# Two-block transformer on one core: the second block's norms, output projections and routing rearranged

## What is computed

```python
h = concat(meta, x)                                  # (272, 1024)
for i in range(2):
    if i == 0:                                       # short convolution
        b, c, u = split(rmsnorm(h, g_mix[0]) @ w_in, 3)
        h = h + (b * conv3(c * u)) @ w_out
    else:                                            # latent attention, 8 heads
        a = rmsnorm(h, g_kv) @ w_dkv                 # keys and values
        cq = rmsnorm(rmsnorm(h, g_mix[1]) @ w_dq, g_cq)
        h = h + attention(cq @ w_uq, a, w_ukv) @ w_o
    h = h + hier_moe(rmsnorm(h, g_ffn[i]))           # 64 experts in 8 groups
return rmsnorm(h, g_final)[:, 16:]

def hier_moe(x):       # x (272, 1024)
    # logits = x @ [w_grp, w_exp] (72 columns): the best group of 8, in it the best 2 experts
    # each expert: (silu(x @ w_gate) * (x @ w_up)) @ w_down, hidden width 256, 3 MB of weights
```

## Time and profile before

| | us |
|---|---|
| median of 3 runs | 2895.99 (2892.11 to 2897.56) |
| the profiled execution | 2896.46 |
| its span | 2894.7 |
| TensorE busy in the span | 2553.1 (88%) |
| VectorE busy | 701.9 (24%) |
| ScalarE busy | 346.7 (12%) |

### The profile page before, as it was taken

One profiled execution on the slowest core, in us unless ns is written; L12 is line 12 of the kernel. 1 busy time (PEld: TensorE's weight loads), 2 busy tenths in 40 slices (PEclk: granted clock), 3 DMA queues, 4 the chain that ended last, 5 costly groups with the idle time before them and its releaser, 6 DMA issues.

```text
span 2894.7 us, 30016 instructions
## 1 busy us (share of the span) xinstructions
PE 2553.1 (88%) x11566; PEld 1550.9 (54%) x11566; DVE 701.9 (24%) x1516; ACT 346.7 (12%) x770; POOL 35.7 (1%) x57
## 2 busy tenths in 40 slices
PE   7999779998999968999897888889869869888887
PEld 5776447774777545777573433434335534443433
DVE  1111521112111352111222323232221133223232
ACT  2001211002000222000200011111102100111011
POOL 0000000000000000000000000000000000000000
PEclk9999879999999968999998799999977678999999
DMA  8432405434552322342514499999740046999995
GB/s 283 160 131 102 146 0 175 149 116 150 177 174 102 133 85 88 131 165 102 168 59 174 198 422 422 422 421 422 312 154 1 1 181 289 422 422 422 422 422 224
DMA packets 206424, 618.45 MB, mean 214 GB/s; under 512 B 14941, under 2 KB 122150, under 8 KB 156950
## 3 DMA queue, kind: packets, MB, share of 16 engines
q1 hardware_dynamic: 200022, 610.89, 54.5%
q0 software_dynamic: 1600, 5.06, 0.5%
q10 hardware_dynamic: 4736, 1.58, 0.2%
HBM read 616.44 MB, written 1.05 MB: 213 GB/s over the span
## 4 chain that ended last, share of the span: by engine, by line
issue 68%; PE 14%; DMA 11%; DVE 2%; PEld 1%; POOL 1%; SPq 1%; ACT 1%; DVEq 0%; ACTq 0%; POOLq 0%; PEldq 0%
DMA ring<-expert_parts 11%; PE PS L1051 3%; PE PS L1127 3%; PE PS L1071 1%; PE PS L1100 1%; PE PS L596 1%; PEld PS L1071 1%; SPq L761 1%; PE PS L543 1%; POOL small L1243 1%; PE PS L578 1%; PE PS L1116 1%; PE PS L579 1%; PE PS L1823 1%; ACT xn L1286 0%
## 5 line engine op out<-in xcount | busy, mean ns | idle before, releaser
L1862 PE MATMUL PS<-xT,ring 128*128 128x256 f32 x2816 | 628.8, 382 | 11.7 <-DVE xT L1526 9.8
L1862 PEld LDWEIGHTS PS<-xT,ring 128*128 128x128 f32 x2816 | 538.8, 192 | 121.2 <-issue 49.1
L1127 PE MATMUL PS<-ring,arena 128*32 128x512 f32 x2048 | 269.7, 676 | 82.2 <-DMA ring<-expert_parts 79.4
L1872 PE MATMUL PS<-ring,arena 128*128 128x512 f32 x704 | 316.1, 592 | 0.0
L1100 PE MATMUL PS<-arena,xn 128*128 128x128 f32 (+1 forms) x1632 | 298.0, 313 | 6.8 <-DVE arena L993 6.8
L1100 PEld LDWEIGHTS PS<-arena,xn 128*128 128x128 f32 (+1 forms) x1632 | 236.3, 195 | 98.4 <-issue 37.3
L1127 PEld LDWEIGHTS PS<-ring,arena 128*32 128x32 f32 x2048 | 70.0, 122 | 273.1 <-issue 168.3
L1547 DVE TENSOR_TENSOR arena<-PS,rb 128x256 f32<-128x256 f32 x88 | 37.4, 425 | 726.3 <-PE PS L1862 725.6
L1116 PE MATMUL PS<-arena 128*128 128x512 f32 (+1 forms) x408 | 199.1, 610 | 7.8 <-DVE h L1009 5.2
L1872 PEld LDWEIGHTS PS<-ring,arena 128*128 128x128 f32 x704 | 133.4, 190 | 132.9 <-issue 126.7
L1009 DVE TENSOR_TENSOR h<-h,PS 128x1024 f32<-128x1024 f32 (+1 forms) x102 | 123.9, 1215 | 309.5 <-PE PS L1116 309.5
(11 more groups left out here) (310 smaller groups left out, 1722.2 us busy)
## 6 DMA issues: line engine op xcount, KB each, us to landing
ring<-expert_parts SPq DMA_DIRECT2D x384, 1024.0 KB, 15.5
ring<-ffn_gate_up SPq DMA_DIRECT2D x88, 1024.0 KB, 7.6
ring<-ffn_down SPq DMA_DIRECT2D x44, 1024.0 KB, 9.8
ring<-w_in SPq DMA_DIRECT2D x16, 768.0 KB, 5.3
ring<-conv_w_in SPq DMA_DIRECT2D x12, 1024.0 KB, 11.7
ring<-w_out SPq DMA_DIRECT2D x8, 768.0 KB, 5.8
ring<-ple_gate SPq DMA_DIRECT2D x8, 768.0 KB, 5.6
rows<-norm_gains POOLq DMA_DIRECT2D x8, 512.0 KB, 8.6
```

The costliest lines, as they stand in the source:

```text
L1127: last = mm(PS[BLK * j:BLK * (j + 1), 2, :], lhsT=xgT[:, k, j * BLK:(j + 1) * BLK], rhs=gu[j][:, k, :], start=k == 0, stop=k == KD - 1)
L1862: last = mm(PS[:, 4 + local % 4, s * 256:(s + 1) * 256], lhsT=w[:, s, k, j * P:(j + 1) * P], rhs=xT[:, k, META:T2], start=k == 0, stop=k = ...
L1872: return mm(PS[:, 2 * t + n, :], lhsT=hid[:, j, t * P:(t + 1) * P], rhs=w[:, j, n * 512:(n + 1) * 512], start=first, stop=final, skip_grou ...
```

## The change

1. Transposes take raw rows of `h` in halves (`h2_turn`), as the halves are updated; ScalarE and VectorE copy them with the gain (`h2_copied`, `meta_copied`, `last_quarter`). 1/rms (`h2_rstd`) is applied to the products: the convolution's by a spread row vector `rb3` and its square `rb3sq`, the latents and the logits by a scalar per row.
2. The output projections (`out_projection`, `out_act`, `out_vec`) work tile by tile. The meta rows' 16 products are made on four column strips of 32 and folded by two products with a constant. The logits are made inside, between the transposes.
3. The scaled rows for the selection are written by ScalarE after the logits' inputs are made; features are in plain order for the logits.
4. Counts take four wider products in place of nine, with two sums by VectorE. The copy of gathered rows is in halves.
5. After each expert loop the combines use banks of their own; in the last layer the meta tile is left out, and squares, 1/rms, scaling and store go tile by tile.

```diff
+        def h2_copied(b, turned_at, t, n, bank, gain):
+            act = nc.scalar
+            act.wait_ge(S.h2_turned, H2_TURNED[b] + turned_at)
+            for k in range(4):
+                last = act.activation(xT[:, 4 * n + k, xcol(t)], PS[:, bank, k * P:(k + 1) * P], ACT.Copy,
+                                      scale=gain[:, 4 * n + k:4 * n + k + 1])
+            last.then_inc(S.h2T_act, 1)
+        def h2_square(b, half_at, t, n):
+            act = nc.scalar
+            if half_at is not None:
+                act.wait_ge(S.h2_half, H2_HALF[b] + half_at)
+            pr, c = (META, slice(0, D)) if t == 2 else (P, slice(512 * n, 512 * n + 512))
+            return act.activation(xn[0:pr, t, c], h[0:pr, t, c], ACT.Square, scale=1.0 / 32, accum_out=ssq[0:pr, n, t:t + 1])
+        def meta_copied(dve, b, turned_at, bank, outs):
+            dve.wait_ge(S.h2_turned, H2_TURNED[b] + turned_at)
+            for dst, gain in outs:
+                last = nc.vector.tensor_tensor(dst[:, :, 0:META], PS[:, bank, 0:KD * META].rearrange("p (k w) -> p k w", w=META),
+                                               gain.unsqueeze(2).to_broadcast([P, KD, META]), ALU.mult)
+            last.then_inc(S.h2T_vec, 1)
+        def last_quarter(dve, b, turned_at, gain):
+            dve.wait_ge(S.h2_turned, H2_TURNED[b] + turned_at)
+            nc.vector.tensor_tensor(xT[:, 4:8, xcol(1)], PS[:, 3, :].rearrange("p (k w) -> p k w", w=P),
+                                    gain[:, 4:8].unsqueeze(2).to_broadcast([P, 4, P]), ALU.mult).then_inc(S.h2T_vec, 1)
+        def h2_rstd(dve, b, r):
+            dve.wait_ge(S.h2_sq, b + 1)
+            nc.vector.scalar_tensor_tensor(ms[:, 0:3], ssq[:, 0, :], EPS, ssq[:, 1, :], ALU.add, ALU.add).then_inc(S.ms_ready, 1)
+            dve.wait_ge(S.rstd_ready, r + 1)
+        def h2_turn(b, t, n, bank, half_at):
+            pe = nc.tensor
+            if b:
+                pe.wait_ge(S.h2_half, H2_HALF[b] + half_at)
...
+                for k in range(4):
+                    last = pe.transpose(PS[:, bank, k * P:(k + 1) * P], h[:, t, (4 * n + k) * P:(4 * n + k + 1) * P], ident)
+            last.then_inc(S.h2_turned, 1)
+        def out_projection(pe, i, src, slots):
...
+            for n in range(2):
+                products(0, n, range(KD - 1))
+            if i == 0:
+                pe.wait_ge(S.conv_ready, KD)
+            for n in range(2):
+                products(0, n, [KD - 1]).then_inc(S.out_done, 1)
+            for n in range(2):
+                for c in range(2):
+                    for j in range(4):
+                        last = mm(PS[32 * j:32 * j + 32, 4 + n, :], lhsT=src[:, 2 * j + c, 0:32], rhs=w[n][:, 2 * j + c, :],
+                                  start=c == 0, stop=c == 1)
+                        if n == c == 1:
+                            last.then_inc(S.strips_done, 1)
+            products(1, 0, range(KD)).then_inc(S.out_done, 1)
+            pe.drain().then_inc(slot_free[i][slots[0]], 1)
+            pe.wait_ge(S.const2_loaded, 16)
+            pe.wait_ge(S.strips_copied, i + 1)
+            for n in range(2):
+                last = mm(PS[0:META, 6 + n, :], lhsT=cst("fold"), rhs=strips[:, n, :], start=True, stop=True)
+            last.then_inc(S.out_done, 1)
+            for n in range(2):
+                h2_turn(b, 0, n, n, n + 1)
+            products(1, 1, range(4))
+            h2_turn(b, 2, 0, 6, 4)
+            h2_turn(b, 1, 0, 2, 3)
+            products(1, 1, range(4, KD)).then_inc(S.out_done, 1)
+            pe.drain().then_inc(slot_free[i][slots[1]], 1)
+            pe.wait_ge(M[i].router_loaded, 48)
+            pe.wait_ge(S.h2T_act, H2T_ACT[b] + 2)
+            logits(0)
+            pe.wait_ge(S.h2T_vec, H2T_VEC[b] + 1)
+            logits(2)
+            pe.wait_ge(S.h2T_act, H2T_ACT[b] + 3)
+            h2_turn(b, 1, 1, 3, 5)
+            logits(1, range(4))
+            pe.wait_ge(S.h2T_vec, H2T_VEC[b] + 2)
+            logits(1, range(4, KD)).then_inc(M[i].pe_step, 1)
...
         def second_act(act, norm):
             act.wait_ge(S.h_upd, 9)
             act.dma_start(const2, A["const_table2"]).then_inc(S.const2_loaded, 16)
             router_loads(act, 0)
-            norm(8, 3)
+            gain = cols("norm_mix_g_2", 8)
+            for u, (t, n) in ((1, (0, 0)), (2, (0, 1)), (4, (1, 0))):
+                h2_copied(0, u, t, n, 2 * t + n, gain)
+            for t in range(2):
+                act.wait_ge(S.h_half, 16 * DEPTH + 2 * t + 2)
+                for n in range(2):
+                    h2_square(0, None, t, n)
+            h2_square(0, None, 2, 0).then_inc(S.h2_sq, 1)
...
             def gathered(n):
-                dve.wait_ge(M[i].selected, n + 1)
-                v_.tensor_tensor(xgT, PS[:, 0:2, :].rearrange("p a (k w) -> p (a k) w", w=P),
-                                 gk.unsqueeze(2).to_broadcast([P, KD, P]), ALU.mult).then_inc(M[i].xgT_ready, 1)
+                for half in range(2):
+                    ks = slice(HALF * half, HALF * half + HALF)
+                    dve.wait_ge(M[i].selected, 2 * n + half + 1)
+                    v_.tensor_tensor(xgT[:, ks], PS[:, half, :].rearrange("p (k w) -> p k w", w=P),
+                                     gk[:, ks].unsqueeze(2).to_broadcast([P, HALF, P]), ALU.mult).then_inc(M[i].xgT_ready, 1)
...
-            for t in range(3):
-                combine(groups, t)
+            pe.wait_ge(M[i].xgT_ready, 2 * groups + 2)
+            for t, bank in ((0, 6), (1, 0), (2, 2))[0:3 - i]:
+                combine(groups, t, bank)
```

More of the change, by code:

```diff
@@ L425, in build @@
         convT = take(2180, [KD, T2])
+        rb3, rb3sq = arena[:, 4400:4400 + T2], arena[:, 4672:4672 + T2]
+        diag3 = take(4944, [3, P])
+        strips = take(5400, [2, 512])
         wr = take(11400, [KD, NG + NE])
@@ L432, in build @@
         e1, e2, msel, rsel, ta, tb = [take(1100 + 192 * i, [3, NE]) for i in range(6)]
+        sums = take(1100 + 192 * 2, [5, NE])
         thr = take(2252, [NE, 8])
@@ L787, in experts, with second_pool @@
             return groups
[L789 to L798 removed]
+        def second_pool(pool, rstd, power):
+            for r in range(28, 34):
+                rstd(r, 3)
+            for t in range(2):
+                power(34 + t, rs[:, t:t + 1], ms[:, t:t + 1], 1)
+        H2_HALF = {1: 0, 2: 5, 3: 10, 4: 15}
@@ new lines, in out_projection, with products, logits @@
+        def out_projection(pe, i, src, slots):
+            mm = nc.tensor.matmul
+            b = 2 * i + 1
+            w = [slot_w(j, KD, 512) for j in slots]
+            def products(t, n, ks):
+                for k in ks:
+                    last = mm(PS[:, 2 * t + n, :], lhsT=src[:, k, xcol(t)], rhs=w[n][:, k, :], start=k == 0, stop=k == KD - 1)
+                return last
+            def logits(t, ks=range(KD)):
+                r = META if t == 2 else P
+                for k in ks:
+                    last = mm(PS[0:r, 4, t * (NG + NE):(t + 1) * (NG + NE)], lhsT=xT[:, k, xcol(t)], rhs=wr[:, k, :],
+                              start=k == 0, stop=k == KD - 1)
+                return last
+            for n in range(2):
[35 more added lines that the diff above has]
+            logits(1, range(4, KD)).then_inc(M[i].pe_step, 1)
@@ new lines, in out_act @@
+        def out_act(act, i, gain):
+            b = 2 * i + 1
+            act.wait_ge(S.strips_done, 4 * i + 4)
+            nc.scalar.activation(strips, PS[:, 4:6, :], ACT.Copy).then_inc(S.strips_copied, 1)
+            for n in range(2):
+                h2_square(b, n + 1, 0, n)
+            for n in range(2):
+                h2_copied(b, n + 1, 0, n, n, gain)
+            h2_square(b, 3, 1, 0)
+            h2_square(b, 4, 2, 0)
+            h2_copied(b, 4, 1, 0, 2, gain)
+            h2_square(b, 5, 1, 1).then_inc(S.h2_sq, 1)
@@ L1052, in second_pe @@
                                   start=k == 0, stop=k == KD - 1)
+                    if x == 0 and s == 1:
+                        pe.wait_ge(S.diag_ready, 3 * DEPTH + 1)
+                        for t in range(3):
+                            r = META if t == 2 else P
+                            spread_ = mm(PS[:, 7, xcol(t)], lhsT=cst("ones")[0:r, :], rhs=diag3[0:r, t, 0:r], start=True, stop=True)
+                        spread_.then_inc(S.r_done, 1)
                 last.then_inc(S.conv_products, 1)
@@ L1435, in _ @@
                 ple(l)
-            second_act(act, norm, squares)
+            second_act(act, norm)
         @block.vector
```

296 lines of the change are left out of this document (173 added, 123 removed).

## The result

The changed kernel takes 2811.24 us (median of 4 runs, 2807.77 to 2813.31), the kernel before 2894.05 us in the same comparison: ratio 0.9715, 95% interval 0.9695 to 0.9734. The forecast was 2818 in 2800 to 2838, and faster. The profiled execution took 2813.31 us with a span of 2811.6, against 2896.46 and 2894.7: 83.1 us of span to explain, and I forecast 78.

What follows compares the result with a forecast made beforehand. Expert-weight DMA was taken to bound the loops, so only the serial stretches around them gain. Terms summed to 80.2 us, less 2 for hops gives 78; from the median 2895.99 that forecasts 2818 us, range 2800 to 2838.

Steps and rivals of the forecast that it cites:

- The frame: Loops and first block: DMA sets the loops' length, they stay unchanged, and time saved before or between them counts in full.
- A: Entry of the second block: products start 7.0 us earlier, less 1.0 for the spread and 3 for clock; gain 3 us.
- B: First output projection, last convolution product to last logit: 70.8 us become 43, a gain of 27.8 us (21 to 29).
- D: Second output projection up to the last logit: 66.1 us become 43, a gain of 23.1 us (16 to 24).
- C: Routing in both layers: fewer count instructions and a shorter wait before the expert products, a gain of 3.4 us.
- E: Attention's entry: products start 13.6 us earlier and first ones run 2.3 faster at 2.4 GHz; gain 15.9 us (11 to 16).
- F: Tail: no meta tile, norm and store tile by tile, half the bytes in the last store; gain 7 us (6 to 7.6).
- hops: Whole change: 2 us taken off the summed gain for hops between engines that could not be placed.
- Rival 1: Same mechanism, clock worse placed, logits at 0.50 in both layers: 19 us less gain, about 2837; chance 0.15.
- Rival 2: Routing: first selections run at 2.4 GHz, 15.06 to 8.4 us a layer, 13 us more gain, 2805 or less; chance 0.08.

## Why the prediction was right, point by point

The time was 6.8 us below the forecast and inside the range. The frame and most terms were right; that the sum of the terms, 80.2, came out as 80.8 is partly luck, since misses of 2.4 and 0.4 below and of 1.2, 1.1, 0.6 and 0.55 above nearly cancel. Each step against the stages above:

| step | predicted | measured |
|---|---|---|
| A entry and cold convolution | 3 | 7.15 - 3.6 = 3.55 |
| B first projection | 27.8 | 28.9 |
| D second projection | 23.1 | 22.7 |
| C routing, two layers | 3.4 | 2.24 + 2.36 = 4.6 |
| E attention's entry | 15.9 | 13.0 + 0.46 = 13.5 |
| F end | 7 | 7.6 |
| sum | 80.2 | 80.8 |
| hops | -2 | none seen |
| loops, rest of the attention, first block | 0 | -0.2 + 2.1 + 1.4 - 0.9 = 2.4 |

- **The frame was right.** Time between the loops counted in full. The first loop got 0.2 us longer and the second 2.1 shorter, which is what loops with the same code do (468.9 to 473.7 over all such traces), and of 56 us of added work all but 2 to 4 vanished in them. The last row of the table, 2.4 us that the forecast had at nothing, is this scatter and that of the attention.
- **A.** Products began 11.01 us after the first block's end, at 1418.41 with the block ending 0.9 later than before; predicted 1417.6. They did begin at 0.50, as said: 16 products in 10.28 us, where the kernel with added products took 7.60. The convolution grew by 3.6, of which the spread is 0.93. The 4 taken off were nearly right.
- **B and D.** 43 was predicted for both, 41.9 and 43.4 came. Strips 3.64 (3.5), fold 1.88 (1.75), logits 3.08 + 2.06 = 5.14 at clock 1.00 (5.1). The hops of 0.6 and the late 1/rms of 0.8 don't stand before the last logit, which the first stage missed 43 by. In D they don't either. There the first 16 products took 15.69 us instead of the 14.0 reckoned, at half clock for a while, and this 1.7, which the sum had at nothing, took their place: D came out near 43 by luck. Rival 1 needed the logits at 0.50, and that fell with the gaps.
- **C.** From the first count to the selection 10.41 us against 12.49: the counts gave the 2.0 predicted. From the selection to the first expert product 14.95 against 16.46, 1.5 less where 0.5 was predicted: the wait of 1.40 went entirely, since the first half of the gathered rows is copied while TensorE selects the second and the expert products start with that half. The wait ahead of the counts grew from 7.02 to 8.37, 1.35: here stand the two sums, the third scaled copy (0.8 together by the prediction) and the late 1/rms, which B had counted ahead of the last logit. In sum 2.24 instead of 1.7 in the first layer.
- **C, ScalarE's part.** The scaled rows "wanted 20 us later" and the exponential "wanted after some 6 us of VectorE work" were right in order and left the price out. The three strided passes take 6.17 us, 2.06 each, where ScalarE's pass over as many elements at the end takes 1.06. The exponentials were done at 1561.84 and VectorE took them up at 1561.94. It cost nothing by 1.3 us in the first layer, not by a comfortable margin.
- **E.** The step that failed is the sentence "With the gap gone they should run at 2.4 GHz, 2.3 more". The start came 13.0 earlier (13.6 said, with w_dq as what is late next, and that is what the row names in eight of the ten traces below). But the first 8 products (16 instructions; the prediction calls them 16 products) took 6.27 us after 2.6 us of transposes and a wait of 1.64: the clock was still 1.00 in that wait, fell 0.3 us into the products and stayed at 0.50 for 3.4 us. The gap had become shorter and had not gone. The sentence beside it on the Trainium skill, "TensorE: Matmul & The Clock Gate", Part 4 (PE-mode transpose), that transposes don't count as busy, had given 13.6, and this trace came out by it. It isn't the whole story. In the kernel before, the clock rose at the block's entry within 1423 to 1424 us, behind 24 transposes and nothing else, and of the ten traces without added products at that place five show 6.26 or 6.27 us and five 4.57 or 4.58, behind waits of 1.48 to 2.63 us, both the shortest and the longest among the quick ones. One program gave both (6.27 above, 4.57 in its second run). Timeline of TensorE in that second run:

```profile
2070.07 4.57 PE L1268 MATMUL PS<-ring,rows 128*128 128x320 f32 x16 [1.54 <-DVE rows L839]
```

So the term of 2.3 should have been a chance of about one half. With two unread products in the gap it was 4.57 each of two times.

- **F.** 7.6 against 7, the upper bound of its range; undoing it gave 7.3. The last store was issued at 2808.6 and the span ended 3.0 us later, just under the 3.1 to 4.4 that I allowed.
- **Rival 2**, the selections at 2.4 GHz, was put at 0.08 since "VectorE's chain of small steps still leaves TensorE without work for 7 us before the counts". That is what happened: 15.03 us in both layers of every trace in which the routing's gaps were not filled. Once they were, the gain was there, 7.5 us in each layer of the kernel with all gaps filled.

## What to carry to other kernels

Find first which stretches end on DMA: cut there, and cost only what lies between. In this kernel 56 us of TensorE work inside such a stretch cost 2 to 4, and the strips, the counts and the end, outside it, were paid in full.

A gap of TensorE costs itself, and it can cost the work behind it half its speed. Here three gaps of 16 us in all made 8.5 us of selections into 15.0. Products that nobody reads, placed in gaps whose length is known from a trace, and four DMA issues moved out of a critical engine's way took back some 23 to 26 us, over a quarter of what the whole rewrite gave. They must be shorter than the gap at half speed too, or they become the wait.

An idle time whose releaser reads "issue" on an engine that starts DMAs deserves a look at its queue rows: 3.2 us stood there.

A stage that nobody edited can move by more than the change under test: the attention took 177.8 us in one trace and 169.3 in another with the same code. Collect each stage from every trace before a gain in it is put down to an edit.

## What the runs showed of the hardware

- 16 products of 16 rows by 512 columns take 13.91 us whole and 3.64 us as strips, 32 columns of the array each: 3.8 times less, before the fold of 1.88 us.
- A ScalarE pass over 128x1024 whose reads step by eight elements (a copy with a scale, L986) takes 2.06 us; one that reads in order (the squares, L971) takes 1.06.
- The granted clock fell to 0.50 in the attention's scores. Windows of the changed kernel:

```profile
2160.00:2161.00 1.00, 0.51 (x3) 0.30 (x2) 0.00 (x0) 0.85 (x3) 0.00 (x0) 1.00 0.00 0
2161.00:2162.00 1.00, 1.00 (x4) 0.70 (x4) 0.00 (x0) 0.83 (x1) 0.00 (x0) 0.57 0.03 8
```

TensorE had been busy without a break from 2144 to 2160, the last 2.2 us of it with transposes (L574), and was idle for 0.49 us only, while waits of 1.5 to 2.6 us at the attention's entry left the clock up in five of ten traces. So the length of the last gap alone doesn't decide it. What does stays open: 24 wider products in the attention put the fall off and didn't prevent it.

- Whether the clock falls in a gap of some 2 us is not the same from one execution of a program to the next. The Trainium skill, "TensorE: Matmul & The Clock Gate", Part 1 (The HAM clock gate), says that the monitor runs free of the kernel and that the count of slow products varies by run. The five and five traces agree that it varies; that the free-running monitor is the reason, no run here shows.
